# Projections stream 512 weight columns into a bank per token tile, with token tile 0 ahead at block ends

## The chip, the cores and the metric

The kernel runs on one core of a Trainium2 chip. The metric is device time in microseconds of one execution. The names of engines are those of the profile: PE is TensorE (PEld its weight loads), ACT is ScalarE, DVE is VectorE, POOL is GpSimd and SP is SyncE, which issues the DMAs (SPq is its queue).

## The reference

Two layers run one after the other on x of 256 tokens by 1024 channels. Four token mixers (a: gated DeltaNet with a convolution, b: neighbourhood attention, c: grouped attention, d: mLSTM) share one input projection. The matrix products that the change touches are these:

```python
for l in range(DEPTH):                                   # 2 layers
    h = _rms(x, norm_g[l])
    p = jnp.einsum('bsd,de->bse', h, w_in[l])            # 256 x 1024 times 1024 x 11808
    ...                                                  # p is split among the mixers, their z gates and the merge gates
    y_a, y_b, y_c, y_d = ...                             # four mixers, 256 x 512 each
    ys = jnp.stack([y_a, y_b, y_c, y_d], axis=2)
    proj = jnp.einsum('bsnw,nwd->bsnd', ys, w_branch[l]) # 512 x 1024 for each mixer
    gates = jax.nn.sigmoid(gate_logits.reshape(B, S, N_BRANCH, D_MODEL))
    merged = jnp.sum(gates * proj, axis=2)
    x = x + jnp.einsum('bsd,de->bse', merged, w_out[l])  # 1024 x 1024
```

## The kernel before, in words

**Number format.** Each float32 weight and activation is split into a rounded high part and a low rest, both in the format fp32r. A product (`split_product`, L626 to L632) is three matmuls into the same PSUM bank: high by high (L630), high by low (L631), low by high (L632).

**Weights.** Weights come as units of 128 x 512 numbers, 256 KB. SP loads a unit into one of 4 slots of `ring`. ACT rounds it to `w_high` (`split`, L1098), DVE subtracts to `w_low` (L1407), and `w_split` is raised. There are 4 slots of `w_high`/`w_low` too. PE raises `weights_used` after the last matmul of a unit; ACT's split of unit u waits for that of unit u - 4, and SP's load of unit u waits for `w_split` of unit u - 4.

**Blocks.** A block is 4 units. A projection block (za, c, zc, b, zb, d, o, zd, gate, out) makes 256 output columns for both token tiles (t = 0, 1, of 128 tokens): a unit holds 2 k-tiles of 256 columns, and each gives 2 k-tiles x 2 token tiles x 3 = 12 matmuls with an activation tile of 128 x 128 as the stationary operand and 256 weight columns as the moving one. Both token tiles share one bank, and one instruction takes it out. A branch block makes 512 columns of a mixer's product, in two halves of 256, with a bank per token tile. Convolution blocks (conv) have the weights stationary and 256 tokens moving.

**Order.** `order()` writes out by hand one list of steps which every engine runs in its own program order. The streamed blocks stand between the steps of the mixers. In each step of a block ACT and DVE first split the 4 units that come 4 units later (the next block's), and then ACT (or DVE) takes the block's own bank out. The banks are pj0 and pj1 in turn; from the gate blocks on pj0, pj1 and mb5 in turn. At the end of a layer, `merge_turn` transposes the merged result on PE (L624), ACT and DVE split it into `h_high`, `h_low` (L1363, L1823), and the out blocks read that.

Of the kernel before, what the change touches and what calls it, by code (L numbers as in the profile page):

```python
# [52 lines left out]
WB = 256  # L53
UK, UN = 2, 4
# [71 lines left out]
def order():  # L126
# [3 lines left out]
    def proj(kind, n):  # L130
        return [("proj", kind, i) for i in range(n)]

    def gates(n):
        return [g for c in range(2) for g in (("proj", "gate", (n, c, 0)), ("proj", "gate", (n, c, 1)), ("branch", n, c))]

    streamed = iter(proj("za", 2) + proj("c", 4) + proj("zc", 2) + proj("b", 6) + proj("zb", 2) + proj("d", 4)
                    + proj("o", 2) + proj("zd", 2) + [g for n in BRANCHES for g in gates(n)])
    o = []

    def stream():  # L140
        step = next(streamed, None)
        if step and step[:2] == ("proj", "gate") and step[2][1:] == (0, 1):
            o.append(("y_parts", step[2][0]))
        if step:
            o.append(step)
        return step
# [56 lines left out]
    return o[:-1] + [("merge_turn", 0), ("merged", 0), o[-1], ("merged", 1)] + proj("out", 4)  # L203


def weight_plan(stages):
# [3 lines left out]
    for name, *args in stages:  # L210
        if name == "branch":
            plan.append(("branch", tuple(args), args[1] * 512))
        elif name == "proj" and args[0] == "gate":
            n, c, i = args[1]
            plan.append(("gate", args[1], GATES + n * D + c * 512 + WB * i))
        elif name == "proj":
            plan.append((args[0], args[1], first[args[0]] + WB * args[1]))
# [3 lines left out]
def build(nc, x_in, norm_g, w_in, conv_a, dn_a_log, dn_dt_bias, dn_norm_g, na_q_norm, na_k_norm, na_rpb,  # L221
          ga_q_norm, ga_k_norm, ml_i_bias, ml_f_bias, ml_norm_g, w_branch, w_out, table, out):
    ctx = ExitStack()
    with ctx:
# [37 lines left out]
        w_high, w_low = sb("w_high", PARTS, UK, WB), sb("w_low", PARTS, UK, WB)  # L262
        ring = sb("ring", RAW, UK, WB)
# [144 lines left out]
        def room(bank, key):  # L408
# [3 lines left out]
            if key[0] not in ("pj", "branch"):  # L412
                bank.signals += 1
# [99 lines left out]
        merge_done = sem("merge_done")  # L513

# [45 lines left out]
        z_order = [a[1:] for a in stages if a[0] == "proj" and a[1] in ("za", "zb", "zc", "zd")]  # L560
        z_no = {a: n for n, a in enumerate(z_order)}
# [12 lines left out]
        product_banks, turn = {}, 0  # L574
        for a in stages:
            if a[0] == "branch" or a[:2] in (("proj", "gate"), ("proj", "out")):
                n = NT if a[0] == "branch" else 1
                product_banks[a] = [(pj + mb[5:])[(turn + t) % 3] for t in range(n)]
                turn += n
            elif a[0] == "proj":  # L580
                product_banks[a] = [pj[turn % 2]]
                turn += 1

        def run(split=None, **steps):


            for name, *args in stages:
                if split and name in ("proj", "branch"):
                    n = block_no[(args[0], args[1])] if name == "proj" else block_no[("branch", tuple(args))]
                    for u in range(UN * n + PARTS, min(UN * (n + 1) + PARTS, UN * len(plan))):  # L590
                        split(u)
                if name in steps:
                    steps[name](*args)
# [21 lines left out]
        with nc.Fori(0, DEPTH) as layer:  # L615
            with nc.Block() as block:
                @block.tensor
                def _(pe):
# [45 lines left out]
                    def proj(kind, arg):  # L664
                        n = block_no[(kind, arg)]
                        b = product_banks[("proj", kind, arg)][0]
                        if kind == "out" and arg == 0:
                            pe.wait_ge(*released(("mT", 1, 0)))
                        pe.wait_ge(*room(b, ("pj", kind, arg)))
                        for u in range(UN):  # L670
                            unit = UN * n + u
                            if kind == "out" and arg == 0 and u == UN // 2:

                                merged_turn(1)
                                pe.wait_ge(*released(("mT", 1, 1)))
                            if kind == "conv" and arg == 0:
                                pe.wait_ge(h_split, 2 * (u * UK // 4) + 2)
                            pe.wait_ge(w_split, unit + 1)
                            for i in range(2):
                                o = b.t[:, i * WB:(i + 1) * WB]  # L680
                                for k in range(UK):
                                    w = [v[:, unit % PARTS, k] for v in (w_high, w_low)]
                                    h = [v[:, u * UK + k] for v in (h_high, h_low)]

                                    flags = dict(start=(u == 0 and i == 0 and k == 0), stop=(u == UN - 1 and k == UK - 1))
                                    sl = slice(i * P, (i + 1) * P)
                                    if kind == "conv":
                                        last = split_product(o, [v[:, sl] for v in w], h, **flags)
                                    else:
                                        last = split_product(o, [v[:, sl] for v in h], w, **flags)  # L690
                            last.then_inc(weights_used, 1)

# [241 lines left out]
                    def d_prep():  # L934
                        for t in range(NT):
                            pe.wait_ge(*released(("pj", "d", 3)))
# [62 lines left out]
                    def branch(n, c):  # L999
                        pe.wait_ge(y_split, BRANCHES.index(n) + 1)  # L1000
                        banks = product_banks[("branch", n, c)]
                        for u in range(UN):
                            half, k0 = u // 2, (u % 2) * UK
# [1041 lines left out]
```

## Time and profile before

| | |
|---|---|
| median of 3 runs | 1118.13 us (1106.73 to 1119.17) |
| profiled execution, first to last instruction | 1107.8 us |
| its own whole time | not given apart; 1118.13 is 10.3 above the span |
| PE, share of the span busy with matmuls | 87% (x9686) |
| DVE, ACT, POOL | 63%, 48%, 24% |
| mean granted TensorE clock | 0.947 |
| ring loads, issue to landing | 3.2 us median for 256 KB |

A share is the time in which at least one instruction of the engine was under way. Matmuls overlap, so the mean duration of one is longer than the distance between two.

### The profile page before, as it was taken

Reading aid. Unit: us, or ns where it says so; the run is one execution under the profiler, and the core shown is the slowest. Engines: PE = TensorE matmul, PEld = TensorE weight load, DVE = VectorE, ACT = ScalarE, POOL = GpSimd, SP = SyncE. Lnnn points to the kernel's source line nnn. Section 1 sums busy time; section 2 is a strip of 40 time slices with the busy share of each in tenths; the row PEclk is TensorE's granted clock in tenths of the full one; section 3 lists DMA queues with packets and bytes.
Section 4 is the critical chain, followed back from the end, with each engine's and each line's share of the span. In section 5 each row is a group of like instructions: output and inputs, shape, how many; then the busy total and the mean of one; then the engine's idle time right before and its main releaser. Section 6 shows DMA issues by size and latency. Waiting matters only on the chain.

```text
span 1107.8 us, 24699 instructions
## 1 busy us (share of the span) xinstructions
PE 958.4 (87%) x9686; PEld 912.4 (82%) x9686; DVE 693.9 (63%) x1145; ACT 536.9 (48%) x1050; POOL 264.5 (24%) x268
## 2 busy tenths in 40 slices
PE   4889889889888898999868898898997889989987
PEld 3889779788787798899868887797887878989987
DVE  3977765446368676576468767563562786765663
ACT  3775444444344555554357654444433445554552
POOL 1452112232323013111034501121431320231110
PEclk9989899989999998999968998899999989999998
DMA  7544645425274344456255455553244642444653
GB/s 190 159 137 122 148 104 123 108 62 138 66 155 125 110 119 114 136 161 200 78 134 153 115 140 124 120 118 102 79 116 105 153 123 79 129 119 135 174 169 115
DMA packets 159935, 139.98 MB, mean 126 GB/s; under 512 B 30910, under 2 KB 158150, under 8 KB 159686
## 3 DMA queue, kind: packets, MB, share of 16 engines
q1 hardware_dynamic: 152630, 137.34, 46.8%
q10 hardware_dynamic: 7184, 1.02, 0.6%
q8 instruction: 78, 1.28, 0.5%
q14 instruction: 43, 0.35, 0.1%
HBM read 135.17 MB, written 6.82 MB: 128 GB/s over the span
## 4 chain that ended last, share of the span: by engine, by line
PE 32%; DVE 7%; ACT 4%; DMA 3%; issue 2%; POOL 1%; ACTq 1%; SPq 0%; DVEq 0%; POOLq 0%
PE pj L630 7%; PE pj L632 6%; PE pj L631 6%; DMA ring<-in_w_in 3%; DVE w_low L1407 2%; PE mb L630 1%; PE mb L632 1%; PE mb L631 1%; ACT w_high L1098 1%; PE pair L624 1%; ACT big L1103 1%; PE pair L797 1%; PE mb L930 0%; PE mb L849 0%; PE pair L792 0%
## 5 line engine op out<-in xcount | busy, mean ns | idle before, releaser
L1407 DVE TENSOR_TENSOR w_low<-ring,w_high 128x512 fp32r<-128x512 f32 x464 | 348.1, 772 | 238.5 <-ACT w_high L1098 237.3
L1098 ACT ACTIVATE w_high<-ring 128x512 fp32r<-128x512 f32 x464 | 287.8, 630 | 358.7 <-PE pj L632 228.4
L630 PE MATMUL pj<-w_high,h_high 128*128 128x256 f32 x1184 | 353.5, 299 | 29.4 <-DVE w_low L1407 29.2
L631 PE MATMUL pj<-w_low,h_high 128*128 128x256 f32 x1184 | 344.7, 291 | 0.0
L632 PE MATMUL pj<-w_high,h_low 128*128 128x256 f32 x1184 | 344.4, 291 | 0.0
L630 PEld LDWEIGHTS pj<-w_high,h_high 128*128 128x128 f32 x1184 | 237.4, 201 | 36.9 <-issue 24.0
L631 PEld LDWEIGHTS pj<-w_low,h_high 128*128 128x128 f32 x1184 | 237.7, 201 | 0.6 <-issue 0.5
L632 PEld LDWEIGHTS pj<-w_high,h_low 128*128 128x128 f32 x1184 | 237.1, 200 | 0.0
L1103 ACT ACTIVATE big<-pair 128x512 f32<-128x512 f32 (+2 forms) x136 | 60.3, 482 | 17.4 <-PE pair L624 8.1
L630 PE MATMUL mb<-w_high,h_high 128*128 128x256 f32 x224 | 65.6, 293 | 3.1 <-DVE h_low L1823 3.1
L631 PE MATMUL mb<-w_low,h_high 128*128 128x256 f32 x224 | 64.4, 287 | 0.0
L632 PE MATMUL mb<-w_high,h_low 128*128 128x256 f32 x224 | 64.4, 287 | 0.0
L630 PE MATMUL pj<-h_high,w_high 128*128 128x256 f32 x192 | 56.9, 297 | 5.5 <-DVE h_low L1421 5.3
L2006 POOL TENSOR_TENSOR zbuf<-zbuf,mid 128x512 f32<-128x512 f32 x20 | 28.2, 1431 | 134.6 <-DVE mid L1810 134.6
L631 PE MATMUL pj<-h_low,w_high 128*128 128x256 f32 x192 | 56.1, 292 | 0.0
L632 PE MATMUL pj<-h_high,w_low 128*128 128x256 f32 x192 | 55.9, 291 | 0.0
L1905 POOL TENSOR_TENSOR big<-big,tab 128x256 f32<-128x256 f32 x40 | 31.4, 805 | 97.7 <-PE pair L781 63.7
L630 PE MATMUL pj<-w_high,y_high 128*128 128x256 f32 x176 | 50.6, 288 | 2.7 <-issue 2.7
L631 PE MATMUL pj<-w_low,y_high 128*128 128x256 f32 x176 | 49.8, 283 | 0.0
L632 PE MATMUL pj<-w_high,y_low 128*128 128x256 f32 x176 | 49.7, 283 | 0.0
L630 PEld LDWEIGHTS mb<-w_high,h_high 128*128 128x128 f32 x224 | 44.2, 198 | 4.3 <-DVE h_low L1823 3.6
L631 PEld LDWEIGHTS mb<-w_low,h_high 128*128 128x128 f32 x224 | 44.1, 197 | 0.0
(276 smaller groups left out, 1719.6 us busy)
## 6 DMA issues: line engine op xcount, KB each, us to landing
ring<-in_w_in SPq DMA_DIRECT2D x368, 256.0 KB, 3.2
ring<-in_w_branch SPq DMA_DIRECT2D x64, 256.0 KB, 3.0
ring<-in_w_out SPq DMA_DIRECT2D x32, 256.0 KB, 3.0
big<-skew SPq DMA_DIRECT2D x32, 128.0 KB, 4.4
skew<-in_na_rpb SPq DMA_DIRECT2D x16, 224.0 KB
out_x<-btm SPq DMA_DIRECT2D x12, 256.0 KB, 3.8
btm<-out_x SPq DMA_DIRECT2D x8, 256.0 KB, 5.1
tab<-in_table SPq DMA_DIRECT2D x1, 1408.0 KB, 7.9
```

The source lines that it names most:

```text
L624: last = tr(bank.t[0:width, k * P:(k + 1) * P], v, ident)
L630: mm(o, r32(a), r32(b), start=start, stop=False, skip_group_check=True)
L631: mm(o, r32(a), r32(b_low), start=False, stop=False, skip_group_check=True)
L632: return mm(o, r32(a_low), r32(b), start=False, stop=stop, skip_group_check=True)
L797: last = mm(b.t[rows_of(r), c:c + C], sT1[rows_of(r), j, h], xt_of(s)[rows_of(r), h], start=True, stop=True)
L1098: f(r32(w_high[:, u % PARTS]), ring[:, u % RAW], ACT.Copy).then_inc(w_rounded, 1)
L1103: f(dst, view(bank_of(key).t), ACT.Copy, scale=scale).then_inc(bank_of(key).free, 1)
L1407: tt(r32(w_low[:, u % PARTS]), ring[:, u % RAW], w_high[:, u % PARTS], ALU.subtract).then_inc(w_split, 1)
L1905: pool.tensor_tensor(sLm[:, j].rearrange("p (k h) n -> p k h n", k=2), sLT[:, j].rearrange("p (k h) n -> p k h n", k=2), both, ALU.mult)\
L2006: pool.tensor_tensor(m, m, gact[i % 2][:, t], ALU.add).then_inc(merge_done, 1)
```

## The change

All projections but the convolution's now work on 512 output columns at once. A unit is one k-tile of 512 columns, a block of 512 columns is 8 units in two parts of 4, and each token tile has a bank of its own. A product is again three matmuls, now with 512 moving columns. At the first and the last pair of units of a block, token tile 0 takes both units before token tile 1 does; between them the tiles alternate unit by unit. `front_done` is raised when token tile 0 is complete, so that its bank can be taken out while tile 1 goes on. ACT and DVE take the banks out one by one, between the splits. The convolution keeps its units (2 k-tiles of 256 columns), with banks pj0, pj1, pj0, pj1, mb4, mb5. At the end of a layer the first 4 units of out go ahead of `merge_turn` 1 instead of the first 2. `b_out` uses mb4 instead of mb5. The number of units and their size, so the number of splits and loads, stay as they are.

```diff
-WB = 256
-UK, UN = 2, 4
+CW, CK = 256, 2
+WB, UN = 512, 4
...
-    return o[:-1] + [("merge_turn", 0), ("merged", 0), o[-1], ("merged", 1)] + proj("out", 4)
+    last = proj("out", 2)
+    return o[:-1] + [("merge_turn", 0), ("merged", 0), o[-1], last[0], ("merge_turn", 1), ("merged", 1)] + last[1:]
...
+        product_banks, front_no, turn = {}, {}, 0
+        for name, *args in stages:
+            if name == "proj" and args[0] == "conv":
+                product_banks[("conv", args[1])] = [(pj + pj + mb[4:])[args[1]]]
+                continue
+            if name == "branch":
+                key = ("branch", tuple(args))
+            elif name == "proj" and args[1][1] == 0:
+                key = (args[0], args[1][0])
+            else:
+                continue
+            late = name == "branch" or args[0] in ("gate", "out")
+            product_banks[key] = [(pj + mb[5:])[(turn + t) % 3] if late else pj[t] for t in range(NT)]
+            turn += NT if late else 0
+            front_no[key] = len(front_no) + 1
...
+                    def token_products(kind, block, n, k0, depth, tokens):
+
+                        banks = product_banks[(kind, block)]
+
+                        def product(t, u):
+                            if k0 + u == 0:
+                                pe.wait_ge(*room(banks[t], ("pj", kind, block, t)))
+                            w = [v[:, (UN * n + u) % PARTS] for v in (w_high, w_low)]
+                            h = [v[:, k0 + u, t * P:(t + 1) * P] for v in tokens]
+                            last = split_product(banks[t].t, h, w, k0 + u == 0, k0 + u == depth - 1)
+                            if t == NT - 1:
+                                last.then_inc(weights_used, 1)
+                            elif k0 + u == depth - 1:
+                                last.then_inc(front_done, 1)
+
+                        for u in range(0, UN, 2):
+                            if k0 + u in (0, depth - 2):
+                                for v in range(2):
+                                    pe.wait_ge(w_split, UN * n + u + v + 1)
+                                    product(0, u + v)
+                                product(1, u)
+                                product(1, u + 1)
+                            else:
+                                for v in range(2):
+                                    pe.wait_ge(w_split, UN * n + u + v + 1)
+                                    product(0, u + v)
+                                    product(1, u + v)
...
+                        block, part = arg
+                        if part == 0 or kind == "out":
+                            for u in due:
+                                split(u)
+                            return
+                        for u in due[:2]:
+                            split(u)
+                        act.wait_ge(*front(kind, block))
+                        evict(kind, block, 0)
+                        for u in due[2:3]:
+                            split(u)
+                        act.wait_ge(*products_done(kind, arg))
+                        evict(kind, block, 1)
+                        for u in due[3:]:
+                            split(u)
...
-                    def branch(n, c):
+                    def branch(n, c, due):
+                        for u in due:
+                            split(u)
                         i = branch_no[(n, c)]
-                        dve.wait_ge(*products_done("branch", (n, c)))
-                        dve.wait_ge(*released(("pj", "gate", (n, c, 1))))
-                        for t in range(NT):
-                            b = bank_of(("branch", n, c, t))
+                        for t in range(NT):
+                            dve.wait_ge(*(front("branch", (n, c)) if t == 0 else products_done("branch", (n, c))))
+                            dve.wait_ge(*released(("pj", "gate", (n, c), t)))
+                            b = bank_of(("pj", "branch", (n, c), t))
```

On ACT, at the first gate block of the last mixer (mixer d, output columns 0 to 511), before. `weights_used` is PE's count of finished units, `ring_full` a DMA's landing:

```order
L1098 ACTIVATE w_high<-ring 128x512 [waits weights_used,ring_full0]
L1098 ACTIVATE w_high<-ring 128x512 [waits weights_used,ring_full1]
L1098 ACTIVATE w_high<-ring 128x512 [waits weights_used,ring_full2]
L1098 ACTIVATE w_high<-ring 128x512 [waits weights_used,ring_full3]
L1156 ACTIVATE mid<-pj0 128x2x256 [waits merge_done,pj1_free,weights_used]
```

The same place of the changed kernel (the second part of that gate block):

```order
L1128 ACTIVATE w_high<-ring 128x512 [waits weights_used,ring_full0]
L1128 ACTIVATE w_high<-ring 128x512 [waits weights_used,ring_full1]
L1175 ACTIVATE mid<-pj0 128x512 [waits merge_done,pj0_free,front_done]
L1128 ACTIVATE w_high<-ring 128x512 [waits weights_used,ring_full2]
L1175 ACTIVATE mid<-pj1 128x512 [waits merge_done,pj1_free,weights_used]
L1128 ACTIVATE w_high<-ring 128x512 [waits weights_used,ring_full3]
```

The bank of token tile 0 is taken out before the third split, that of tile 1 before the fourth.

On PE, from the last product of a branch block (mixer d, columns 0 to 511) into the gate block behind it, before. `pj1_free` says that the bank is taken out; the bank mb5, which the branch block's tile 0 has filled, is asked for again one block of 48 matmuls later:

```order
L630 MATMUL pj0<-w_high,y_high 128x256
L631 MATMUL pj0<-w_low,y_high 128x256
L632 MATMUL pj0<-w_high,y_low 128x256
L630 MATMUL pj1<-w_high,h_high 128x256 [waits w_split,pj1_free]
L631 MATMUL pj1<-w_low,h_high 128x256
L632 MATMUL pj1<-w_high,h_low 128x256
```

The same place of the changed kernel:

```order
L646 MATMUL pj0<-w_high,y_low 128x512
L644 MATMUL pj1<-w_high,h_high 128x512 [waits pj1_free,w_split]
L645 MATMUL pj1<-w_low,h_high 128x512
L646 MATMUL pj1<-w_high,h_low 128x512
L644 MATMUL pj1<-w_high,h_high 128x512 [waits w_split]
L645 MATMUL pj1<-w_low,h_high 128x512
L646 MATMUL pj1<-w_high,h_low 128x512
L644 MATMUL mb5<-w_high,h_high 128x512 [waits mb5_free]
```

Bank mb5, filled by tile 0 of the branch block, is now asked for 6 matmuls after that block's end.

## Rows read from the trace of the kernel before

**Rows 1.** The page: busy time, share of the span and instructions of each engine.

```profile
PE 958.4 (87%) x9686; PEld 912.4 (82%) x9686; DVE 693.9 (63%) x1145; ACT 536.9 (48%) x1050; POOL 264.5 (24%) x268
```

**Rows 2.** Span and mean granted clock of the core.

```profile
core 0: 1107.8 us, clock 0.947
```

**Rows 3.** Groups of PE's instructions by line, shapes apart: busy us, mean ns, idle before.

```profile
L630 PE MATMUL pj<-w_high,h_high 128*128 128x256 f32 x1184 | 353.5, 299 | 29.4 <-DVE w_low L1407 29.2
...
L630 PE MATMUL mb<-w_high,h_high 128*128 128x256 f32 x224 | 65.6, 293 | 3.1 <-DVE h_low L1823 3.1
...
L630 PE MATMUL pj<-w_high,y_high 128*128 128x256 f32 x176 | 50.6, 288 | 2.7 <-issue 2.7
...
L630 PE MATMUL mb<-w_high,y_high 128*128 128x256 f32 x80 | 23.6, 295 | 0.0
```

**Rows 4.** Timeline, a block at full clock: start us, duration us, instruction.

```profile
400.07 0.28 PE L630 MATMUL pj<-w_high,h_high 128*128 128x256 f32 x1
...
400.19 0.28 PE L631 MATMUL pj<-w_low,h_high 128*128 128x256 f32 x1
...
400.31 0.28 PE L632 MATMUL pj<-w_high,h_low 128*128 128x256 f32 x1
```

**Rows 5.** Timeline of PE, a block at half clock.

```profile
423.22 0.41 PE L630 MATMUL pj<-w_high,h_high 128*128 128x256 f32 x1
423.43 0.41 PE L631 MATMUL pj<-w_low,h_high 128*128 128x256 f32 x1
```

**Rows 6.** Timeline of PE: plain float32 matmuls of 256, 512 and 128 moving columns.

```profile
157.92 1.03 PE L881 MATMUL mb<-mid 128*128 128x256 f32 x4
...
351.28 1.88 PE L954 MATMUL pair<-mid,tab 128*128 128x512 f32 x4
...
185.71 1.05 PE L894 MATMUL mb<-mid 128*128 128x128 f32 x8
```

**Rows 7.** The instructions of L881, L954 and L894: duration ns min/median/max.

```profile
L881 PE MATMUL mb<-mid x32: 377/379/634, 153.2 to 729.2; 128*128 128x256 f32 x32
...
L954 PE MATMUL pair<-mid,tab x16: 590/592/1062, 343.3 to 903.1; 128*128 128x512 f32 x16
...
L894 PE MATMUL mb<-mid x64: 270/275/377, 166.3 to 740.8; 128*128 128x128 f32 x64
```

**Rows 8.** The waits of PE, by what ended them: us in total, times, longest us.

```profile
PE pj L630 <- DVE w_low L1407: 29.2, 18, 4.8
...
PE pair L781 <- POOL big L1905: 9.8, 7, 3.4
...
PE mb L630 <- DVE h_low L1823: 3.1, 2, 1.6
...
PE pair L624 <- DVE zbuf L1816: 2.1, 2, 1.0
```

**Rows 9.** Issues of ring loads, median us to landing: 345 to 440, then 305 to 345, then 100 to 150.

```profile
ring<-in_w_in SPq DMA_DIRECT2D x31, 256.0 KB, 3.0
...
ring<-in_w_in SPq DMA_DIRECT2D x12, 256.0 KB, 4.5
...
ring<-in_w_in SPq DMA_DIRECT2D x20, 256.0 KB, 6.7
```

**Rows 10.** The page: issues by line, KB each, median us to landing.

```profile
big<-skew SPq DMA_DIRECT2D x32, 128.0 KB, 4.4
skew<-in_na_rpb SPq DMA_DIRECT2D x16, 224.0 KB
```

**Rows 11.** Waits of ACT for ring loads: us in total, times, longest us.

```profile
ACT w_high L1098 <- DMA ring<-in_w_in: 86.3, 52, 4.4
```

**Rows 12.** Timeline around the end of a branch block (its last matmul starts at 483.26).

```profile
482.27 2.73 DVE L1407 TENSOR_TENSOR w_low<-ring,w_high 128x512 fp32r<-128x512 f32 x4
...
483.26 0.28 PE L632 MATMUL mb<-w_high,y_low 128*128 128x256 f32 x1
...
483.64 0.63 ACT L1098 ACTIVATE w_high<-ring 128x512 fp32r<-128x512 f32 x1 [0.23 <-PE mb L632]
...
484.91 0.68 DVE L1810 SCALAR_TENSOR_TENSOR mid<-mid,pj 128x512 f32<-128x512 f32 x1
...
485.51 0.68 DVE L1810 SCALAR_TENSOR_TENSOR mid<-mid,mb 128x512 f32<-128x512 f32 x1
```

**Rows 13.** Timeline of ACT and DVE in a gate block whose bank L1156 takes out.

```profile
491.37 0.63 ACT L1098 ACTIVATE w_high<-ring 128x512 fp32r<-128x512 f32 x1 [0.81 <-PE pj L632]
491.91 0.58 ACT L1156 ACTIVATE mid<-pj 128x512 f32<-128x512 f32 x1
492.04 0.69 DVE L1407 TENSOR_TENSOR w_low<-ring,w_high 128x512 fp32r<-128x512 f32 x1 [0.75 <-ACT w_high L1098]
```

More of the change, by code:

```diff
@@ L572, in build, with front @@
         diag += [us[:, s].rearrange("p h n -> p (h n)")[:, 0:H * C] for s in (2, 3)]
[L574 to L582, printed above, removed]
+        product_banks, front_no, turn = {}, {}, 0
[13 more added lines that the diff above has]
+            front_no[key] = len(front_no) + 1
+        def front(kind, block):
+            return front_done, front_no[(kind, block)]
         def run(split=None, **steps):
@@ L678, in proj @@
                             pe.wait_ge(w_split, unit + 1)
                             for i in range(2):
[L680 to L690, printed above, removed]
@@ L693, in a_turn, with proj @@
+                    def proj(kind, arg):
+                        if kind == "conv":
+                            conv_product(arg)
+                            return
+                        block, part = arg
+                        if kind == "out" and block == 0:
+                            pe.wait_ge(*released(("mT", 1, part)))
+                        token_products(kind, block, block_no[(kind, arg)], UN * part, KT, (h_high, h_low))
                     def a_turn(q):
@@ new lines, in residual, with proj @@
+                    def residual(block, t):
+                        b = bank_of(("pj", "out", block, t))
+                        v = x[:, t, block * WB:(block + 1) * WB]
+                        tt(v, v, b.t, ALU.add).then_inc(b.free, 1)
+                    def proj(kind, arg, due):
+                        if kind == "conv" or arg[1] == 0 or (kind[0] != "z" and kind != "out"):
+                            for u in due:
+                                split(u)
+                            return
+                        block = arg[0]
+                        for u in due[:2]:
+                            split(u)
@@ new lines, in proj @@
+                            residual(block, 0)
+                        else:
+                            z_gate(kind, 0)
+                        for u in due[2:3]:
+                            split(u)
+                        if kind == "out":
+                            dve.wait_ge(*products_done(kind, arg))
+                            residual(block, 1)
+                        else:
+                            z_gate(kind, 1)
+                        for u in due[3:]:
+                            split(u)
```

221 lines of the change are left out of this document (108 added, 113 removed).

## The prediction

> **What bounds the kernel now.** I read the page's first part first: PE is busy 87% of the span, DVE 63%, ACT 48% [rows 1], so PE is the engine to watch. Its groups by line [rows 3] show where its work is. The projections that change have 1184 + 224 + 176 + 80 = 1664 matmuls on L630, and as many on L631 and L632: 4992 in all. Group means (about 290 ns) are latencies. What a matmul costs is the distance between two starts: 0.12 us at full clock [rows 4], so 4992 x 0.12 = 599 us, more than half of the span. Then I read what PE waits for [rows 8]: the longest item is w_low, 29.2 us in 18 waits; all others are small. So most of the time PE issues one matmul behind the other, and their distance sets the end, except where weights come late.
>
> **Part 1: 512 columns in a matmul, the main term.** The 4992 matmuls become 2496 of 512 columns. The trace has no fp32r matmul of 512 columns, so I bound its distance from its neighbours. At half clock (1.2 GHz) 256 columns stand 0.21 us apart [rows 5], which is 256 / 1.2 = 213 ns: one column a cycle and nothing else. At 2.4 GHz this would be 107 ns, but [rows 4] have 120: 13 ns more. What adds them? Plain float32 matmuls show it. Four of 256 columns span 1.03 us and one lasts 379 ns [rows 6, 7], so they stand (1.03 - 0.38) / 3 = 0.217 apart; 512 columns (1.88 - 0.59) / 3 = 0.43. So plain float32 takes two cycles a column, 512 cycles for 256 columns: 213 ns and some 3 more. Each of these loads its own 128 x 128 stationary tile, as ours do. Plain float32 with 128 columns (256 cycles, as many as ours) stands (1.05 - 0.275) / 7 = 0.11 apart [rows 6, 7]. So there is a floor of 110 to 120 ns that a weight load behind each matmul seems to set; it lies over 107 ns of columns and vanishes under 213. A 512-column fp32r matmul streams for 512 cycles, like L881, so I take 216 ns, its row being the nearest. Upper bound: the 13 ns stay with every matmul, 213 + 13 = 227. Farthest bound: it costs by the column, 2 x 120 = 240, no gain. Below 213 the half-clock row excludes. By 216 two old matmuls (240 ns) become 24 ns cheaper: 2496 x 24 = 60 us. At half clock two times 213 become 427, no gain; the mean clock of 0.947 [rows 2] means that up to 10.6% of the time is at half, much of it idle. I take 4 us off: **-56 us**. By 227 the same step gives 2496 x 13 = 32, less 2.
>
> The Trainium skill (TensorE: Matmul & The Clock Gate, section "Back-to-back issue gap") gives N / 2.4 + 2.5 ns at full clock: 109 for 256 columns and 216 for 512. By this rule alone a pair would save 2 x 109.2 - 215.8 = 2.6 ns, 6.5 us in all, and the change would be worth nothing. The trace disagrees with it at 256 columns (120) and agrees at 512 cycles (217). The same page's section "LDWEIGHTS" gives P / 1.2, 107 ns for 128 columns, as the time of a weight load, which would be the floor that the rows show.
>
> **Part 2: where a faster PE gains nothing.** A wait that ends when a load lands keeps its end, however fast PE came to it. There are 18 waits for w_low [rows 8]. Loads take 4.5 and 6.7 us in two stretches instead of 3.0 [rows 9], since the loads through skew stand in the same queue [rows 10]; there mixer steps wait too (L781 7 times, of which I count 4). Each wait cancels the gain of about one block of 4 units, which is 48 x 0.12 - 24 x 0.216 = 0.58 us. With 22 such blocks: **+13 us**.
>
> **Part 3: the weight loop.** Units, splits and loads are as many as before. What changes is how soon they are wanted. A product (3 matmuls) takes 0.65 us. In the new order PE finishes the units of an 8-unit block after products 3, 4, 6, 8, 10, 12, 15 and 16, and starts to need them at 0, 1, 4, 6, 8, 10, 12 and 13. The slot of unit u goes to u + 4, so between release and need lie 5 or 6 products, 3.2 to 3.9 us; before it was 3 units, 4.3 us. The split takes 0.38 from the last matmul's start to ACT, 0.63 on ACT and 0.69 on DVE [rows 12, 13], some 1.7 us. So it fits. The load: from w_split of u to w_split of u + 4 lie 3.0 of landing [rows 9], the two splits and some 0.3 of hand-overs, 4.6 us, against 5.2 that PE now takes for 4 units (5.76 before). It fits with 0.6 to spare: I cost it at nothing. If that cover goes, PE is paced by the ring.
>
> **Part 4: the banks.** Token tile 0 completes 2 products (1.3 us) before the block does, and ACT needs 0.58 for it [rows 13]; behind the waiting ACT stand two splits and the mixers' steps, but both splits before it were free to go earlier. Tile 1 has the next block's first 2 products as cover, 1.3 us. Both fit, for 22 two-part blocks a layer. It does not fit behind a branch block: DVE first makes the split of the last unit, which ends at 485.0 (482.27 + 2.73), and then tile 0's product, 484.91 to 485.59, while PE's stream ended at about 483.38 [rows 12]: 2.2 us later. The next gate block now asks for that bank 6 matmuls in, 1.3 us after the end; before, a whole block (5.76 us) lay between. PE waits 0.9 to 1.0 us where no mixer step stands between: behind the first branch block of mixer c (partly behind its second, where one short step stands) and behind both of mixer d, the last of them before out: 3.5 places a layer, 7 in all: **+7 us**. front_done does not help there, as the four splits stand ahead of it on DVE.
>
> **Part 5: the layer's end.** Before, PE waits 1.0 for zbuf and 1.6 for h_low behind half an out block [rows 8]. Now 4 units of out (5.2 us instead of 2.9) go ahead, and the first wait should go; the second may grow to about 2. **-1 us**. POOL's and SP's orders hold the same instructions.
>
> **Sum:** -56 + 13 + 7 - 1 = -37. The profiled execution has a span of 1107.8 and its own whole time isn't given; 10.3 us lie between span and median, and nothing of the change lies in them. So the span goes to 1071 and the median from 1118.1 to **1081 us**, 0.967 of before. About 2% (22 us) is what a measurement of this kernel can tell from no change.
>
> **The rivals.**
> (a) The 13 ns stay, 227 ns a matmul. The sum is -30 + 7 + 7 - 1 = -17: 1101 us. For it: 120 is 8 to 10 above the 110 of L894, which has as many cycles, so fp32r may add something of its own. Against: at half clock it adds nothing.
> (b) Cost by the column, so the change doesn't give what it is made of: 240 ns, 0 + 7 - 1 = +6: 1124. For it: only fp32r rows could exclude it and there is one width of them. Against: half clock again, where 1.2 GHz is met exactly. The Trainium skill's rule above would end here too (1118 - 6.5 + 6 = 1118), and shares this chance.
> (c) The ring paces PE: if landing rises from 3.0 to 3.9 when asked for faster, the loop is 5.5 us for 4 units and a block gains 0.26 instead of 0.58. -60 x 0.26 / 0.58 = -27, and +6 for half of part 2, +7 - 1: 1103. For it: 4.5 and 6.7 are there [rows 9]. Against: these stretches have other DMAs in the queue.
> (d) Slower: block ends stall. Tile 0's bank is taken out on ACT behind two splits, which wait for ring loads; if a load is late the bank is late, and the next block stands, though its weights are there. Before, the other bank was free. There are 44 two-part and 16 branch block ends. Without part 4 the sum is -44, so it decides from 44 / 60 = 0.73 us an end; with 1.2 us each it is -44 + 72 = +28: 1146. For it: ACT waits 52 times for landings even now [rows 11]. Against: mixer steps stand behind most ends.
>
> **How the numbers follow.** Chances: forecast 0.57, (a) 0.17, (b) 0.08, (c) 0.08, (d) 0.10. The forecast's own spread is some 15 us (part 2 from 6 to 20, part 4 from 2 to 14, half clock). Low end 1062: part 1 whole, parts 2 and 4 at their low ends. High end 1112 takes in (a) and (c) and leaves out (b), (d) and a little below. Faster by over 2% (under 1095.8): nearly all of the forecast and a third of (a) and (c), 0.60. Slower by over 2% (over 1140.5): half of (d), 0.05. The rest 0.35.
>
> **What the profile would show.** Part 1: starts of the 512-column matmuls 0.216 apart (0.227 for (a), 0.24 for (b)), and their count 2496. Part 2: waits for w_low between 25 and 45 us in all. Part 3: no w_low wait in the blocks of stretches with 3.0 us landing. Part 4: PE waits of about 1 us on the third product of a gate block, released by DVE's product of the branch, and none released by ACT's taking out; for (d) these are the many. Part 5: no wait for zbuf. I am wrong if the distance is not 0.216, or if PE's idle time of 149 us (1107.8 - 958.4) grows by more than 35.

## Result and the profile of the changed kernel

The changed kernel takes **1104.37 us** (median of 11 runs, 1099.49 to 1106.40), the kernel before beside it 1115.38 (11 runs). The ratio is 0.9905, 95% interval [0.9877, 0.9933]: it is faster, by 11 us, and not by the 37 that I forecast. The time is inside my range and lies close to the 1101 of rival (a).

Page of the changed kernel, part 1 (against [rows 1]), then its core's row (against [rows 2]):

```profile
PE 932.9 (85%) x7190; PEld 768.2 (70%) x7190; DVE 689.9 (63%) x1145; ACT 539.0 (49%) x1050; POOL 263.1 (24%) x268
```

```profile
core 0: 1098.4 us, clock 0.950
```

PE's busy time falls by 25.5 us and the span by 9.4. So PE's time without work grew from 149.4 to 165.5 us: 16 us of what the matmuls gave are gone in idle time. Groups by line and shape (against [rows 3]; L644 to L646 are now the three matmuls of a product):

```profile
L644 PE MATMUL pj<-w_high,h_high 128*128 128x512 f32 x592 | 249.3, 421 | 42.1 <-DVE w_low L1457 23.0 <-DVE zbuf L1676 9.5 <-ACT mid L1230 6.6
...
L644 PE MATMUL mb<-w_high,h_high 128*128 128x512 f32 x112 | 45.8, 409 | 6.8 <-DVE h_low L1896 3.7 <-DVE mid L1883 1.8 <-DVE zbuf L1883 1.1
```

The idle time before the first group, 29.4 us before the change, is 42.1. Two of its causes are new, zbuf on L1676 and mid on L1230: DVE's z step and ACT's taking out of a bank. The waits of PE say the same (against [rows 8]; us in total, times, longest us):

```profile
PE pj L644 <- DVE w_low L1457: 23.2, 13, 4.8
...
PE pj L644 <- DVE zbuf L1676: 9.5, 4, 3.5
...
PE pj L644 <- ACT mid L1230: 6.6, 2, 3.5
...
PE pj L644 <- DVE mid L1883: 3.0, 4, 0.7
```

The waits for weights shrank (29.2 in 18 to 23.2 in 13), in part because a longer wait for a bank covers them, as experiment 4 shows. On the product's lines all the new waits are for a bank: with the rows `mb` <- mid and zbuf on L1883 (1.8 and 1.1) they come to 22.0 us. The first is at 92 us, in the timeline of the changed kernel (start, duration, instruction, idle time before):

```profile
89.75 0.48 DVE L1534 SCALAR_TENSOR_TENSOR big<-big,small 128x256 f32<-128x256 f32 x1
90.16 1.29 DVE L1457 TENSOR_TENSOR w_low<-ring,w_high 128x512 fp32r<-128x512 f32 x2
...
91.36 0.68 DVE L1676 SCALAR_TENSOR_TENSOR zbuf<-zbuf,pj 128x512 f32<-128x512 f32 x1
...
92.19 0.47 PE L644 MATMUL pj<-w_high,h_high 128*128 128x512 f32 x1 [3.51 <-DVE zbuf L1676]
92.49 0.39 PE L645 MATMUL pj<-w_low,h_high 128*128 128x512 f32 x1
92.72 0.40 PE L646 MATMUL pj<-w_high,h_low 128*128 128x512 f32 x1
92.96 0.39 PE L644 MATMUL pj<-w_high,h_high 128*128 128x512 f32 x1
```

The block of za has filled pj0, and the block of c behind it wants pj0 first. DVE empties it at 91.36, behind a mixer step and two splits that are free to go from 90.16. At its end stands PE, 3.51 us. Two blocks on, at 126.01, it is ACT that keeps the bank:

```profile
118.69 0.62 ACT L1128 ACTIVATE w_high<-ring 128x512 fp32r<-128x512 f32 x1
...
124.75 0.63 ACT L1128 ACTIVATE w_high<-ring 128x512 fp32r<-128x512 f32 x1 [5.44 <-DMA ring<-in_w_in]
125.28 0.58 ACT L1230 ACTIVATE mid<-pj 128x512 f32<-128x512 f32 x1
...
126.01 0.47 PE L644 MATMUL pj<-w_high,h_high 128*128 128x512 f32 x1 [3.16 <-ACT mid L1230]
```

ACT waits 5.44 us for a landing before a split, and the taking out of pj0 stands behind that split: the mechanism of my rival (d), at one place a layer. Both places come again in layer 2 (638.15, 672.22).

The distance of two matmuls can be read in the rows above: 92.49, 92.72, 92.96. It is **0.23 us, not 0.216**. In the whole trace 1546 distances of two such matmuls at full clock are 226 or 227 ns, most others 231 to 236, and 42 are 224. Plain float32 keeps the 216 that I took for it.

### The profile page after: what moved, and what is told of

Same layout as the page of the kernel before. It is cut to its first block and busy times, and to the rows that moved or that the text cites. A ratio compares the mean times of both kernels' runs of the same rounds, so it can differ in the third digit from the quotient of the medians.

```text
span 1098.4 us, 19683 instructions
## 1 busy us (share of the span) xinstructions
PE 932.9 (85%) x7190; PEld 768.2 (70%) x7190; DVE 689.9 (63%) x1145; ACT 539.0 (49%) x1050; POOL 263.1 (24%) x268
## 5 line engine op out<-in xcount | busy, mean ns | idle before, releaser
L644 PE MATMUL pj<-w_high,h_high 128*128 128x512 f32 x592 | 249.3, 421 | 42.1 <-DVE w_low L1457 23.0
L645 PE MATMUL pj<-w_low,h_high 128*128 128x512 f32 x592 | 240.2, 406 | 0.0
L646 PE MATMUL pj<-w_high,h_low 128*128 128x512 f32 x592 | 239.8, 405 | 0.0
L644 PEld LDWEIGHTS pj<-w_high,h_high 128*128 128x128 f32 x592 | 117.3, 198 | 75.9 <-DVE w_low L1457 38.4
L646 PEld LDWEIGHTS pj<-w_high,h_low 128*128 128x128 f32 x592 | 116.8, 197 | 26.5
L645 PEld LDWEIGHTS pj<-w_low,h_high 128*128 128x128 f32 x592 | 117.2, 198 | 23.6
L644 PE MATMUL mb<-w_high,h_high 128*128 128x512 f32 x112 | 45.8, 409 | 6.8 <-DVE h_low L1896 3.7
L646 PE MATMUL mb<-w_high,h_low 128*128 128x512 f32 x112 | 44.4, 396 | 0.0
L645 PE MATMUL mb<-w_low,h_high 128*128 128x512 f32 x112 | 44.2, 394 | 0.0
L644 PE MATMUL pj<-h_high,w_high 128*128 128x256 f32 x128 | 39.0, 305 | 5.8 <-DVE h_low L1471 5.6
L638 PE MATMUL pair<-tab,big 128*128 128x128 f32 x208 | 29.2, 279 | 14.8 <-POOL big L1988 5.1
L646 PE MATMUL pj<-h_high,w_low 128*128 128x256 f32 x128 | 38.3, 299 | 0.0
L644 PE MATMUL pj<-w_high,y_high 128*128 128x512 f32 x88 | 35.2, 400 | 3.3 <-issue 3.3
L646 PE MATMUL pj<-w_high,y_low 128*128 128x512 f32 x88 | 34.4, 391 | 0.0
```

Source lines behind the costliest of these rows:

```text
L638: last = tr(bank.t[0:width, k * P:(k + 1) * P], v, ident)
L644: mm(o, r32(a), r32(b), start=start, stop=False, skip_group_check=True)
L645: mm(o, r32(a), r32(b_low), start=False, stop=False, skip_group_check=True)
L646: return mm(o, r32(a_low), r32(b), start=False, stop=stop, skip_group_check=True)
```

## The experiments

Times are medians beside the ratio to the kernel before in the same session. The changed kernel ran in two sessions, 17 runs with a median of 1103.09 us.

**1. What a matmul costs by its form.** Behind the changed kernel's last product stand ten rows of 32 matmuls on an otherwise idle chip. Two of the ten:

```
+ for i in range(32):
+     mm(o, r(S_[i % 8]), r(W_[i % 4]), start=True, **kw)            # L2107
...
+ for i in range(32):
+     mm(o[:, 0:256], r(S_[i % 8]), r(W_[i % 4][:, 0:256]), start=(i == 0), **kw)   # L2115
```

> The changed kernel with ten rows of 32 matmuls each added behind its last product, on TensorE alone, which measure the distance between matmuls by form (their results are thrown away). Width theory (the product matmul of 512 columns has 213 ns of columns and about 13 ns that no column explains, the 256-column one some 107 and 13): 512 columns with a new stationary operand each time 227 ns, and that whether it accumulates, starts anew or alternates between two banks; 384 columns about 173 ns, 256 about 120 ns. If the 13 ns belong to the load of the stationary operand, 512 columns with the same stationary operand stand 216 ns or less apart; if they belong to the matmul itself, 227 here too. Accumulation theory (the 13 ns are paid for adding onto a bank): 512 columns that start anew stand 216 ns apart and those that accumulate 227. Pause theory (what I forecast, 216 ns in undisturbed stretches, with the 227 caused by the kernel's own traffic on the stationary and moving operands' memory): all rows stand near 216 ns here, where nothing else runs. Plain fp32 at 256 columns 216 ns.

Timeline of this kernel (start, duration of the group, line, shape, count). The first row, L2105, accumulates with a new stationary operand each time; it fell in part into a stretch at half clock and is left out, but the kernel's own products have this form. L2107 starts anew each time, L2109 alternates two banks, L2111 accumulates and keeps the stationary operand; L2113 and L2115 have 384 and 256 columns, all of these fp32r. L2117 and L2119 are plain float32, L2121 and L2123 bfloat16:

```profile
1101.28 7.42 PE L2107 MATMUL pj<-w_high,h_high 128*128 128x512 f32 x32
1108.54 7.42 PE L2109 MATMUL pj<-w_high,h_high 128*128 128x512 f32 x32
1115.79 7.42 PE L2111 MATMUL pj<-w_high,h_high 128*128 128x512 f32 x32
1123.04 5.73 PE L2113 MATMUL pj<-w_high,h_high 128*128 128x384 f32 x32
1128.61 3.99 PE L2115 MATMUL pj<-w_high,h_high 128*128 128x256 f32 x32
1132.44 13.98 PE L2117 MATMUL pj<-tab 128*128 128x256 f32 x64
1146.26 13.98 PE L2119 MATMUL pj<-tab 128*128 128x256 f32 x64
1160.29 6.85 PE L2121 MATMUL pj<-tab 128*128 128x512 bf16 x31
1166.98 3.66 PE L2123 MATMUL pj<-tab 128*128 128x256 bf16 x32
```

A group's start less the one before, by 32: 7.26 / 32 = 227 ns for 512 columns, whatever the bank and the start flag; 5.57 / 32 = 174 for 384; 3.83 / 32 = 120 for 256. The columns alone at 2.4 GHz are 213, 160 and 107: **some 13 ns are left at every width**. Each plain float32 line shows as 64 instructions for 32 matmuls, 13.82 / 64 = 216 ns for an instruction (the counts in [rows 6] and [rows 7] are instructions too), and the 31 distances of bfloat16 at 256 columns give 109. These two forms have some 2.5 ns over their cycles, fp32r 13. So the width theory holds, and the accumulation and pause theories fall.

L2111 doesn't decide whether the 13 ns come from the weight load: its 32 matmuls still load the same tile 32 times. The loads' recorded length doesn't sort the forms either. It is the same for fp32r and plain float32 (groups of the same trace; busy us, mean ns, idle before):

```profile
L2107 PEld LDWEIGHTS pj<-w_high,h_high 128*128 128x128 f32 x32 | 6.0, 188 | 1.2
...
L2117 PEld LDWEIGHTS pj<-tab 128*128 128x128 f32 x64 | 12.1, 190 | 1.6
```

**2. The width undone, all else kept.** Both on the changed kernel (`e_halves`) and on the version of experiment 4 (`b_halves`):

```
- last = split_product(banks[t].t, h, w, ...)
+ for c in range(2):
+     cols = slice(c * CW, (c + 1) * CW)
+     last = split_product(banks[t].t[:, cols], h, [v[:, cols] for v in w], ...)
```

> The changed kernel's order, banks and waits, but each product of 512 columns is issued as two of 256 again, half after half. Width theory: 1776 wide matmuls at 227 ns become 3552 at 120 ns, 13 ns more for each pair, 23 us less what stays hidden behind loads that pace 22 blocks (a sixth), so +19 us: about 1123 us, slower than the kernel before by the 8 us that the new bank waits cost. Order theory (the gain came from the order of the token tiles and the banks, not from the width): 1104 us, no difference from the changed kernel. No part alone: 1115 us, the kernel before's own time, would say that the new bank waits cost nothing.

The 1776 counts only the products into pj at L644; with those into mb and the ones on y it is 2496, and 2496 x 13 = 32 us, 27 by the same sixth.

> The kernel with the edits of the banks and of the branch step (1088 us), but each product of 512 columns issued as two of 256 again. Width theory: as in the undisturbed blocks of the halves on the changed kernel, each block of 512 columns begins 0.28 us later against the rest, about 70 blocks, +20 us: 1106 to 1110 us. Clock theory (in the first test of halves the time rose by 9 us to 12 us and the span times its mean granted clock by 21 us, so that part of the width's gain came back as fewer half-clock stretches): the span times the clock rises from 1036 to 1056 us here too, but the time only to 1097 to 1102 us.

Measured: `e_halves` **1113.27** us, 1.0056 [1.0015, 1.0097], against the changed kernel's 0.9905. It lies halfway between the width theory (1123) and the order theory (1104). `b_halves` **1103.30**, 0.9927 [0.9883, 0.9972], against 0.9771. So by the medians the width is worth 10 and 15 us, by the ratios 0.0151 and 0.0156, some 17. Where nothing waits it shows directly. First matmul of d's first and of its fourth part of 4 units, three parts apart (two blocks of 512 columns have four), in the timelines of the changed kernel and of `e_halves`:

```profile
243.33 0.50 PE L644 MATMUL pj<-w_high,h_high 128*128 128x512 f32 x1
...
265.73 0.50 PE L644 MATMUL pj<-w_high,h_high 128*128 128x512 f32 x1
```

```profile
245.35 0.39 PE L644 MATMUL pj<-w_high,h_high 128*128 128x256 f32 x1
...
268.58 0.39 PE L644 MATMUL pj<-w_high,h_high 128*128 128x256 f32 x1
```

That is 22.40 against 23.23 us: 0.277 for a part of 4 units (the forecast's block), where 24 x 13 ns = 0.31 were expected and my forecast had 0.58. This repeats in nearly every part that waits for nothing. The whole comes to less than 27 us, and two reasons for it stand in the runs. At half clock width gives nothing: rows of the changed kernel in such a stretch stand 0.42 to 0.43 us apart, twice the 0.21 of [rows 5]:

```profile
94.25 0.63 PE L645 MATMUL pj<-w_low,h_high 128*128 128x512 f32 x1
94.68 0.63 PE L646 MATMUL pj<-w_high,h_low 128*128 128x512 f32 x1
95.11 0.63 PE L644 MATMUL pj<-w_high,h_high 128*128 128x512 f32 x1
```

And `e_halves` was granted more clock (median 0.957 against 0.947 for the changed kernel). Span times mean clock, which takes the second effect out roughly, rises from 1042 to 1064 us, by 21. In `b_halves` it rises from 1036 to 1053, by 17, and there the clock hardly differs (0.956 against 0.9545). Within `b_halves` the clock shows by itself: its six runs at 0.952 to 0.963 take 1100 to 1103 us, its three at 0.947 and 0.948 take 1112 to 1114. (In `e_halves` nine runs take 1111 to 1115 us and three 1123 to 1126; two of these three have 0.943 and 0.944, but one has 0.955, so the mean clock doesn't say all.) On the changed kernel the time went as the clock theory has it: the halves were paid back in part by the clock. In the second pair neither theory met the time; 1103.3 lies between their two ranges, and the clock, hardly moved, paid nothing back.

**3. Token tile 0 ahead, undone** (`e_alt` on the changed kernel, `b_alt` on the version of experiment 4):

```
- if k0 + u in (0, depth - 2):
+ if False:
```

> The changed kernel, but the two token tiles alternate k-tile by k-tile to the end of each block, so that tile 0 no longer goes one unit ahead in the first and the last unit. Tile 0 then ends about 0.7 us before the block's end instead of 1.4 us. Bank theory (the first product of the next block waits for tile 0's bank, so every 0.7 us taken from its eviction is added to a wait that exists already): the 12 to 16 places with a bank wait grow by up to 0.7 us each and some 20 more begin to wait a little, +8 to +15 us, 1112 to 1119 us. Rival (evictions have room everywhere, the waits come from splits and loads): within 3 us of 1104.

> The kernel with the edits of the banks and of the branch step (1088 us), with the token tiles alternating to the end of each block. Bank theory (the 11 to 14 us that alternation cost on the changed kernel were evictions of tile 0 that came late, 0.3 to 0.9 us at some 25 places, with the worst of these places now taken away by other banks): 5 to 8 us, 1093 to 1096 us. Rival (its cost has nothing to do with the banks, for example that tile 0's consumers on other engines start later everywhere): as much as before, 1099 to 1102 us.

Measured: `e_alt` **1115.34** us, 1.0007 [0.9973, 1.0041]; `b_alt` **1096.47**, 0.9856 [0.9812, 0.9901]. Alternation costs 12 us on the changed kernel and 8.5 on the other, on the second at the edge of the bank theory's range and under the rival's 11 to 14. In `e_alt` the waits of PE for the z step are 12 instead of 4, and those for the branch step are longer (3.0 and 1.8 us in the changed kernel):

```profile
PE pj L644 <- DVE zbuf L1676: 11.9, 12, 3.5
...
PE pj L644 <- DVE mid L1883: 5.7, 4, 1.4
...
PE mb L644 <- DVE mid L1883: 4.7, 4, 1.6
```

All bank waits together are 30.6 us against 22.0, so 9 of the 12 us are seen as the bank theory has them. In `b_alt` they are 5.0 us in nine against 2.5 in two of `e_both`: there the trace shows only a part of the 8.5 us as bank waits. The mean granted clock was lower as well in both (medians 0.9415 against 0.947, and 0.9495 against 0.9545). How the rest divides stays open. The lead of token tile 0 at the blocks' ends and starts (the edit takes away both) is worth as much as the whole net gain of the change.

**4. The bank waits taken away.** `e_banks` gives the first blocks of c and of zc two idle banks; `e_branch` reads the branch block's banks between the splits; `e_both` does both:

```
+ early = mb[4:] if key in (("c", 0), ("zc", 0)) else pj
- product_banks[key] = [... if late else pj[t] for t in range(NT)]
+ product_banks[key] = [... if late else early[t] for t in range(NT)]
```

```
  def branch(n, c, due):
-     for u in due:
+     for u in due[:2]:
          split(u)
      for t in range(NT):
+         if t == 1:
+             for u in due[2:3]:
+                 split(u)
          ...
+     for u in due[3:]:
+         split(u)
```

> The changed kernel with two edits: the blocks behind the one of za and the last one of c use two other banks, and VectorE's branch step reads tile 0's bank behind the second weight split and tile 1's behind the third, as its z and gate steps do, instead of behind all four. Bank theory: the waits of 3.5 us at the two starts of c and of 3.2 and 3.5 us at the two starts of zc lose their cause, 1.3 + 1.4 us a layer at c and about 0.6 us a layer at zc that was not given back (6 us together), and the waits of 0.75 to 1.1 us behind the branch blocks at six places go, 4 to 5 us: 1093 to 1096 us. Rival (the ring of weight loads paces these stretches, and what is gained at a block's start is waited for at the next landing): 1101 to 1105 us. Second rival (the splits that now stand behind the branch step come too late for TensorE): slower than 1104, up to 1110 us.

> The changed kernel word for word, once more on this chip beside the three edits below, so that their times can be set against its own from the same session. Both theories: 1099 to 1106 us, as before (1104.37 median of 11 runs); an edit that is 1 per cent faster than this is shown faster.

> The changed kernel, but the first blocks of c and of zc use two other banks, nothing else. Bank theory: the waits of 3.5 us at the starts of c (for VectorE's z step, at 92.19 and 638.15 us) and of 3.2 and 3.5 us at the starts of zc (for ScalarE's eviction, at 126.01 and 672.22 us) vanish from the list of TensorE's waits; c(1,1) starts 4.2 us earlier against the rest and zb's second block 2 us earlier in each layer, since a part is waited for again at zc's second block: 4 to 6 us in all, 1098 to 1100 us. Rival (the next load landing is what these stretches wait for in the end): at zb's second block the gain is gone, 1102 to 1105 us.

> The changed kernel, but VectorE's branch step reads tile 0's bank behind the second weight split and tile 1's behind the third, nothing else. Bank theory: the pauses of 0.9 to 1.1 us in the middle of the first unit behind branch(0,0), (2,0), (1,0), (3,0) and (3,1) go in both layers, eight to ten places at 0.8 to 1.05 us: 7 to 9 us in all, 1095 to 1097 us; together with the edit of the banks that is the 16 us which the two gave together. Rival (their sum is not additive, the two together gained by the granted clock, which was 0.954 against 0.947): this one alone gives 4 us or less, 1100 to 1104 us.

Measured, against the changed kernel's 1100.84 (six runs) in their own session: `e_banks` **1093.58** us, 0.9817 [0.9776, 0.9859], so -7.3. `e_branch` **1095.28**, 0.9832 [0.9786, 0.9877], so -5.6. `e_both` **1087.99**, 0.9771 [0.9724, 0.9818], so -12.9 against this run and -15 against the 1103.09 of both sessions. By these medians the two add up; by the ratios they give 0.0078 and 0.0063 together 0.0141 and both at once 0.0124, each ratio with an interval of up to ±0.005, so that additivity is shown only roughly. The ratios' intervals just overlap that of the changed kernel, 0.9895 [0.9851, 0.9940]. In their common session all six runs of `e_banks` (1088 to 1094 us) lie under all six of the changed kernel (1097 to 1106); those of `e_branch` (1090 to 1100) overlap, so that it rests on the trace as much as on its time. `e_both` is 5 us below what was expected; `e_branch` gave less than the 7 to 9 us expected, though more than its rival's 4.

`e_banks` gave more than the 4 to 6 us expected. The bank waits at c and zc are gone, but PE still waits there, now for weights. The first matmul of c, and the waits for w_low on the two kinds of banks:

```profile
89.85 0.50 PE L645 MATMUL mb<-w_high,h_high 128*128 128x512 f32 x1 [2.38 <-DVE w_low L1458]
```

```profile
PE pj L645 <- DVE w_low L1458: 24.9, 13, 4.7
...
PE mb L645 <- DVE w_low L1458: 10.3, 4, 3.1
```

The four waits in the last row are the two starts of c and the two of zc. So a bank wait of 3.5 us is not worth 3.5 us: under it lay one of 2.2 to 2.4 us for weights at c. What the edit gave beyond the difference shows in the windows from 88 to 98 us and from 92 to 98, below those of the changed kernel (columns: stretch, its length, busy us and count of PE, PEld, DVE, ACT, POOL, then PE's granted clock, DMA share, GB/s):

```profile
88.00:98.00 10.00, 6.49 (x25) 5.08 (x24) 9.09 (x18) 3.93 (x8) 0.40 (x1) 0.83 0.38 106
92.00:98.00 6.00, 5.81 (x18) 4.64 (x19) 5.20 (x12) 2.11 (x4) 0.00 (x0) 0.72 0.63 176
```

```profile
88.00:98.00 10.00, 8.15 (x92) 6.84 (x93) 9.24 (x19) 6.06 (x11) 0.24 (x1) 1.00 0.49 146
92.00:98.00 6.00, 6.00 (x84) 5.04 (x83) 5.31 (x12) 3.49 (x6) 0.24 (x1) 1.00 0.66 197
```

With the wait of 3.5 us the clock is granted at half from 93.4 to 96.8, 1.2 us behind its end; c's first part of 4 units takes 6.97 us from its first to its last start instead of 5.34. Without the bank wait it stays at full. This stretch stands at this wait (3.3 to 3.7 us, once 2.3) in both layers of every kernel that keeps the block on pj (the changed kernel and its repeat, `e_branch`, `e_alt`, `e_halves`, and `m_width`, whose second wait is 4.0 us and where it begins 0.3 us before the wait's end), and in none of the five with the other banks (waits of 2.0 to 2.4 us for weights, once 1.0), nor in the kernel before (0.9 and 2.1). So the bank wait costs 1.1 to 1.3 us itself, over the wait for weights, and 1.6 again by the clock, each layer: some 5.6 of the 7.3 us. The rest isn't placed. At zc nearly all is given back: in layer 1 zc starts 3.3 us earlier against c's second block, and its second part of 4 units starts 3.0 of them later again.

In `e_branch` the waits for mid and zbuf on L1883 (5.9 us in eight waits) are gone: no row of PE's waits names the branch step. One such place in both kernels, in the changed one first:

```profile
408.93 0.68 DVE L1883 SCALAR_TENSOR_TENSOR mid<-mid,pj 128x512 f32<-128x512 f32 x1
...
409.66 0.50 PE L644 MATMUL pj<-w_high,h_high 128*128 128x512 f32 x1 [0.75 <-DVE mid L1883]
```

```profile
412.16 0.69 DVE L1886 SCALAR_TENSOR_TENSOR mid<-mid,pj 128x512 f32<-128x512 f32 x1
...
412.64 0.39 PE L644 MATMUL mb<-w_high,y_high 128*128 128x512 f32 x1
```

Tile 0's bank is now read while PE still works on the branch block, 1.2 us before that block's successor starts at 413.32; before it was 1.5 us after.

**5. One more bank wait, with the ring behind it** (`e_more`: `e_both`, and the rotation starts two further, so that gate's first block doesn't want the bank of zd):

```
- product_banks, front_no, turn = {}, {}, 0
+ product_banks, front_no, turn = {}, {}, 2
```

> Both edits of the banks and of the branch step, and the rotation over three banks starts two further, so that the first gate block takes a bank that the block of zd before it does not use. Bank theory: the wait of 1.23 us for VectorE's z step at 322.5 and 861.7 us goes, 0.8 to 1.2 us a layer, about 2 us: 1086 us against 1088 of the two edits alone; in the trace gate's first block starts that much earlier and nothing else moves. Rival (its weights' low halves, which wait for VectorE too, are late by the same amount): no change, 1088 us.

Measured: **1088.14** us, 0.9772 [0.9732, 0.9813], the same as `e_both`. The wait is gone, and counted from the block of zd ahead of it gate's first block starts 1.3 us earlier than in `e_both` in both layers (counted from the span's start, 1.03 and 1.53). By the branch block behind it, two parts of 4 units on, the starts of the two kernels differ by only 0.05 and 0.02 us. In the timelines, a split in gate's second block, first `e_both`, then `e_more`:

```profile
331.27 0.63 ACT L1129 ACTIVATE w_high<-ring 128x512 fp32r<-128x512 f32 x1 [2.02 <-DMA ring<-in_w_in]
...
332.68 0.50 PE L645 MATMUL pj<-w_high,h_high 128*128 128x512 f32 x1 [1.13 <-DVE w_low L1458]
```

```profile
331.21 0.63 ACT L1129 ACTIVATE w_high<-ring 128x512 fp32r<-128x512 f32 x1 [0.98 <-DMA ring<-in_w_in]
...
332.63 0.51 PE L645 MATMUL mb<-w_high,h_high 128*128 128x512 f32 x1 [0.63 <-DVE w_low L1458]
```

The load lands at the same moment in both, and PE goes on at 332.7 and 332.6. The rival holds, though its reason was put loosely: it is the landing, not DVE, that is late by as much. Here a bank wait costs nothing; behind the branch blocks it cost nearly all of itself (5.9 us of waits, 5.6 gained), and at c what it had over the wait for weights, and that again by the clock.

## Why the prediction was wrong, by its steps

**Part 1 failed: "so I take 216 ns, its row being the nearest".** It is 227. My error was to split the 120 ns of 256 columns into a floor of 110 to 120 that columns can cover, and to take plain float32 of as many cycles as the nearest row. The 0.11 us of L894 [rows 6] spoke against a floor of 120 already: it loads a tile of its own each time too. Experiment 1 shows 13 ns over the columns at 256, 384 and 512, for fp32r alone. The upper bound that I had written beside it was the truth: -30 instead of -56. The Trainium skill's rule (TensorE: Matmul & The Clock Gate, section "Back-to-back issue gap"), N / 2.4 + 2.5 ns, fits the bfloat16 rows of experiment 1 (216 and 109), and misses fp32r by some 11 ns at both widths. A pair of narrow matmuls pays its extra twice: joining them saves 13 ns as measured, where that rule had 2.6, and so it spoke too strongly against the change.

**Part 2 (places where a faster PE gains nothing) was right in kind.** Scaled to 0.31 us a part of 4 units its 13 us are 7, so parts 1 and 2 together should have been -23. The halves give 10 to 15 us by the medians, up to 17 by the ratios, and 17 to 21 in span times clock. The rest of the difference to 23 isn't broken down.

**Part 3 holds nearly.** From 345 to 545 us, where loads land in some 3 us, only one wait for weights is left, 0.53 us at mixer d's second gate block (0.75 in layer 2); the two at za (4.8 and 3.0 us) stand there in a stretch with 3.0 us too, but were there before the change. The total of the w_low waits is 23.2 us in 13, just under the 25 to 45 that I gave. That is low because bank waits cover some: in `e_banks` it is 35.2 us in 17.

**Part 4 failed in "both fit, for 22 two-part blocks a layer".** The branch term was right: I forecast 7 us, the waits are 5.9 us, and their removal gave 5.6. Three of the four places a layer are those forecast (behind the first branch block of mixer c and both of d, 0.75 to 0.93 us); the fourth, 0.56 us, is behind mixer a's first. But three other block ends a layer don't fit: za to c, c to zc, and zd to gate. I had priced them at nothing, and taking away the first two gave 7.3 us; the third costs nothing, since a landing ends last there, and in the repeat of the changed kernel it isn't there at all. I had priced the step that empties a bank by its own duration and the two splits before it, and not by the mixer step (za) or the landing (zc) that stands ahead of those in the engine's program order. Nor had I a term for the clock behind such a wait, 1.6 us a layer at c.

**Part 5 holds.** The waits for zbuf at the layer's end are gone, that for h_low is 1.8 instead of 1.6.

With the measured sizes my sum reads -30 + 7 + 13 - 1 = -11, and the medians differ by 11.0. That is luck in good part, and 1104 lies inside my range only because its high end took in the rivals (a) and (c). The fit is better than the terms deserve: the width gave less than 23, and `b_halves`, which has neither the width nor, but for 2.5 us, the bank waits, is at 0.9927 already, some 8 us under the kernel before. What part of the new order gives these 8 us wasn't tried in the old kernel, and stays open.

The 10.3 us between span and median that I carried along are mostly the spread between runs: where a run has both, its whole time is 1.7 to 2.9 us over its span. They don't touch the difference of the two kernels.

**The rivals.** (a) was the case in its mechanism and within 4 us. (b) and (c) fall: 227 isn't 240, and ring loads of the projections land in 3.0 us on the page of the changed kernel, against 3.2 before. (d) exists at 2 of its 60 block ends, with 3.2 and 3.5 us, mostly given back.

## What to carry to other kernels

Before a matmul is widened, measure the distance of two at two widths in its own data type: what is left over the columns, times the number of matmuls that go, is the most that can be gained (here 32 us, of which 10 to 17 came), and another type's rest can mislead (2.5 ns here instead of 13). When each tile goes down to one bank, list for each block end what stands in order ahead of the step that empties it, mixer steps and landings too: here other banks at two places and one step moved between splits gave about as much as the width, and took 1103 to 1088 us, 2.3% under the kernel before. And look first what else ends behind the wait: at c a wait for weights lay under it, and where a load ended last, 1.3 us won were nothing at the next block.

## What the runs showed of the hardware

- An fp32r matmul costs its columns at 2.4 GHz and some 13 ns more (120, 174 and 227 ns for 256, 384 and 512), bfloat16 and an instruction of plain float32 2.5 ns more (216 for 512 cycles, 109 for 256). A plain float32 matmul of 256 columns is two such instructions. At half clock the 13 ns are not there: 213 and 427 ns in the kernels before and after, columns at 1.2 GHz. What they are stays open.
- PE's wait of some 3.5 us in front of c's first block came with a stretch at half clock every time, in twelve places of six traces, and the same block behind a wait of 1.0 to 2.4 us in the five kernels with other banks had full clock. It made that bank wait cost more than twice its own 1.1 to 1.3 us. A wait's length alone doesn't decide: in `e_branch` one of 2.3 us had the stretch behind it, and at 126.01 us in the changed kernel one of 3.16 us had none before 134.4.
- The mean granted clock differed from kernel to kernel, from a median of 0.9415 (`e_alt`) to 0.957 (`e_halves`), and within `b_halves` 0.948 against 0.960 went with some 11 us, as much as the changes that were studied.
